# All first products of the 128 expert blocks ahead of all second products, and 384 gathered tokens in place of 320

## What is computed

```python
q = (xb @ w_query).reshape(PEER_BLOCK, PEER_HEADS, 2, PEER_HALF)
s = jnp.einsum('bhpd,phnd->bhpn', q, sub_keys)
...                                    # top 16 of 128 on each side, top 16 of their 256 sums
eid = e1 * PEER_NKEYS + e2             # 8 heads x 16 experts of 16384, per token
gate = jax.nn.softmax(best_s, axis=-1)
act = jax.nn.gelu(jnp.einsum('bd,bhkd->bhk', xb, expert_u[eid]), approximate=False)
return jnp.einsum('bhk,bhkd->bd', gate * act, expert_v[eid])
```

## Time and profile before

| | us |
|---|---|
| median of three runs | 3494.87 (3494.62 to 3495.22) |
| span of the profiled execution | 3500.7 |
| mixer and projections | 0 to 1197 |
| selection | 1197 to 1635 |
| gate matrices | 1635 to 1877 |
| first group and the others | 1877 to 3471 |
| final norm | 3471 to 3501 |

### The profile page before, as it was taken

One profiled execution on the slowest core, in us unless ns is written; L12 is line 12 of the kernel. 1 busy time (PEld: TensorE's weight loads), 2 busy tenths in 40 slices (PEclk: granted clock), 3 DMA queues, 4 the chain that ended last, 5 costly groups with the idle time before them and its releaser, 6 DMA issues.

```text
span 3500.7 us, 56614 instructions
## 1 busy us (share of the span) xinstructions
PE 3350.9 (96%) x21384; PEld 3291.5 (94%) x21384; DVE 2591.7 (74%) x4995; ACT 1018.7 (29%) x1349; POOL 977.2 (28%) x773
## 2 busy tenths in 40 slices
PE   6999999999998999998998899999999999999996
PEld 6999999899998999998997899999999999999996
DVE  5554444233343379999997899999999999999996
ACT  5742222321322232222543122222222222222222
POOL 0000000000000111111002555555555555555550
PEclk8999999999999999999999999999999999999998
DMA  2111011111322232334889999899998999999992
GB/s 105 40 45 36 29 36 64 68 48 42 141 85 73 89 107 102 106 112 136 266 266 307 333 337 328 318 327 326 338 329 317 327 327 340 328 321 321 329 326 104
DMA packets 304353, 698.46 MB, mean 200 GB/s; under 512 B 23873, under 2 KB 124225, under 8 KB 303201
## 3 DMA queue, kind: packets, MB, share of 16 engines
q0 software_dynamic: 98592, 362.97, 28.5%
q1 hardware_dynamic: 104112, 276.89, 23.3%
q10 hardware_dynamic: 101520, 56.89, 5.3%
...
## 4 chain that ended last, share of the span: by engine, by line
PE 77%; DVE 17%; DMA 2%; DVEq 2%; ACT 1%; issue 1%; ACTq 0%; SPq 0%; PEldq 0%
PE PS L1532 29%; PE PS L365 16%; PE PS L1515 14%; PE PS L1223 6%; PE PS L1253 5%; DVE HOTG L2052 3%; PE PS L1447 3%; PE PS L380 1%; DVE HOT L2048 1%; DVE HOT L2049 1%; DVE fold L1980 1%; DVE besti L1924 1%; DVE sc L1915 1%; DVE besti L1916 1%; DVEq L1978 1%
## 5 line engine op out<-in xcount | busy, mean ns | idle before, releaser
L1532 PE MATMUL PS<-AH,VH 128*128 128x368 f32 x2048 | 513.8, 332 | 20.4 <-DVE VL L2075 10.9
L1532 PE MATMUL PS<-AH,VL 128*128 128x368 f32 x2048 | 515.2, 332 | 0.0
L1532 PE MATMUL PS<-AL,VH 128*128 128x368 f32 x2048 | 509.7, 330 | 0.0
L746 POOL DMA_INDIRECT SLOT<-rows_u,EID x256 | 346.4, 1353 | 578.5 <-DVE XLF L2091 257.5
L746 POOL DMA_INDIRECT SLOT<-rows_v,EID x256 | 333.7, 1304 | 205.7 <-DVE SLOT L2082 167.5
L1532 PEld LDWEIGHTS PS<-AH,VH 128*128 128x128 f32 x2048 | 365.2, 189 | 22.7 <-DVE VL L2075 12.1
L1532 PEld LDWEIGHTS PS<-AL,VH 128*128 128x128 f32 x2048 | 366.2, 189 | 0.0
L1532 PEld LDWEIGHTS PS<-AH,VL 128*128 128x128 f32 x2048 | 365.8, 189 | 0.0
L2091 DVE SCALAR_TENSOR_TENSOR XLF<-SLOT,GA,XLF 128x1024 f32<-128x1024 f32 x256 | 328.0, 1281 | 0.5 <-DMA SLOT<-rows_v,EID 0.2
L1109 ACT ACTIVATE VH<-VRAW 128x512 fp32r<-128x512 f32 x256 | 157.8, 628 | 567.7 <-PE PS L1532 567.7
L2082 DVE SCALAR_TENSOR_TENSOR SLOT<-SLOT,XHF 128x1024 f32<-128x1024 f32 x256 | 312.6, 1221 | 3.3 <-DMA SLOT<-rows_u,EID 3.3
...
## 6 DMA issues: line engine op xcount, KB each, us to landing
RAW<-experts_u SPq DMA_DIRECT2D x128, 512.0 KB, 6.4
VRAW<-experts_v SPq DMA_DIRECT2D x256, 256.0 KB, 5.8
...
RAW<-weights SPq DMA_DIRECT2D x69, 512.0 KB, 3.6
...
```

Source lines behind the costliest of these rows:

```text
L746: pool.indirect_dma_start(out=SLOT[n % NSLOT][:, :], out_offset=None, in_=table, in_offset=bass.IndirectOffsetOnAxis(ap=ids, axis=0)).then ...
L1532: mm = pe.matmul(PS[:, 4 + 2 * (d % 2) + t, 0:CH], w[:, d % 2, c * P:c * P + P], x[:, c, t * CH:t * CH + CH], start=(c == 0 and n == 0), s ...
```

## The change

- The gathered tokens are now 384, three full tiles (NSP = 3); the half tile and all code for it go. The dense ones are 672, in halves of CH = 336. Selection still has nine tiles.
- All 128 u blocks come first: 75 in selection, 43 within the (now 84) steps of the gate stage (up to E1 = 118), 10 in a tail. All activations go to memory.
- Then come 128 units: 16 groups of GE = 8 blocks, with eight second products each. A unit accumulates eight blocks' products, 48 matmuls, before VectorE adds it to HID; three PSUM sets are in turn (SETS). The activations of a group are read back at its predecessor's start (load_raw), and the gates in four parts (load_gates), into buffers that alternate between AHR/ALR and the dense columns of XH/XL. One v block is now 1024 columns wide and takes RAW, WH and WL as a u block does.
- The low parts: GpSimd makes those of all u blocks and of the even units, VectorE those of the odd units.
- The rows are one sequence of 384 u rows and then 384 v rows (NROW). VectorE takes 24 of them in each of the last six tiles of selection (144), two in each gate step (168), 30 in the tail, 28 in each group but the last, and six in the last. SLOTs in turn: four up to the tail, six from there on. The weights are made for half the pairs at a time (GA_CUT).
- The sums of the gathered tokens are transposed in the last group, a tile at a time.
- The loops over groups are written out instead of being a loop in the program.

```diff
-GE = 4
+GE = 8
 NG = NKEYS // GE
-EARLY = 2
-LATE = GE - EARLY
-NE = NG * EARLY
-NSP = 2
-HALF = P // 2
-S0 = NSP * P
-T0 = S0 + HALF
+NSP = 3
+T0 = NSP * P
 ND = T - T0
...
-NSLOT = 5
-NTILE = NSP + 1 + -(-ND // P)
+NTILE = NSP + -(-ND // P)
 PRE = 2
-SEL_E = (4, 5, 5, 5, 5, 5, 5, 5, 5)
+SEL_E = (5, 5, 6, 10, 9, 10, 9, 10, 9)
...
+E1 = 118
...
+NROW = NSP * PAIRS
+TILE_ROWS = 24
+STEP_ROWS = 2
+TAIL_ROWS = (2, 4, 4, 8, 12)
+UNIT_ROWS = (4, 3, 4, 3, 4, 3, 4, 3)
...
+def slot_of(s):
+
+    if s < ROWS_E0:
+        return (L0, L1, QA, QB)[s % 4]
+    if s < ROWS_E1:
+        return (L0, L1, G0, N0)[s % 4]
+    if s < WIDE_FROM:
+        return (L0, L1, N0, N1)[s % 4]
+    return (L0, L1, N0, N1, N2, N3)[(s - WIDE_FROM) % 6]
...
+            def load_unit(n):
+
+                sp.wait_ge(e_lo, n - 1)
+                sp.dma_start(RAW[:, n % 2, :], u_blk[n] if n < NKEYS else v_blk[n - NKEYS]).then_inc(e_in[n % 2], 16)
...
+            for n in range(NKEYS):
+                load_unit(n + 2)
+                sp.wait_ge(e_gelu, n + 3)
+                sp.dma_start(act_dram[n], AS[:, n % 2, :]).then_inc(e_out[n % 2], 16)
+                if n == E1 - 1:
+                    for b in range(2):
+                        sp.wait_ge(w_out[b], 16 * ((NWB + 1 - b) // 2 + 1))
+                    sp.wait_ge(w_mm, NSTEP + 2)
+                    load_raw(0)
...
+            for n in range(NKEYS, UNITS):
+                g, d = divmod(n - NKEYS, KD)
+                if n + 2 < UNITS:
+                    load_unit(n + 2)
+                if g + 1 < NG:
+                    if d == 0:
+                        load_raw(g + 1)
+                    if d in (0, 1, 2, 3):
+                        load_gates(g + 1, d)
...
+            for s in range(NSTEP):
+                for m in range(E0 + 1, E1 + 1):
+                    if s == (e_end(m - 2) + 1 if m > E0 + 1 else 0):
+                        e_low(m)
+                gather_to(ROWS_E0 + STEP_ROWS * s + 4)
...
+            for n in range(NKEYS, UNITS):
+                if n + 1 < UNITS and n + 1 not in LOW_ON_DVE:
+                    e_low(n + 1)
+                gather_to(done + 6)
+                done += UNIT_ROWS[n % KD]
...
+            def v_unit(g, d):
+
+                n, slot = NKEYS + KD * g + d, d % 2
+                hi, lo, at_bank = a_hi(g), a_lo(g), 2 + 2 * SETS[d]
+                pe.wait_ge(e_lo, n + 1)
...
+                for c in range(GE):
+                    if d == 0 and c % 2 == 0:
+                        pe.wait_ge(a_low, GE // 2 * g + c // 2 + 1)
+                    for p, (w, x) in enumerate(((WH, hi), (WH, lo), (WL, hi))):
                         for t in range(2):
...
+            for n in range(NKEYS, UNITS):
+                g, d = divmod(n - NKEYS, KD)
+                last = g == NG - 1
+                if n + 1 in LOW_ON_DVE:
+                    v_low(n + 1)
+                if not last:
+                    if 1 <= d <= 4:
+                        a_gates(g + 1, d - 1)
+                    take(UNIT_ROWS[d])
+                    if d in (6, 7):
+                        for c in range(4 * (d - 6), 4 * (d - 6) + 4, 2):
+                            a_lows(g + 1, c)
...
+                dve.wait_ge(e_mm, n + 3)
+                part = halves(HID[:, d, T0:T])
+                dve.tensor_tensor(part, part, vset(d), ALU.add).then_inc(acc_done, 1)
```

762 lines of the change are left out of this document (299 added, 463 removed).

## The result

The changed kernel takes **3694.02 us** (median of 4 runs, 3686.71 to 3699.91) against 3495.05 us before (median of 4 beside it): a ratio of 1.0569, 95% interval 1.0554 to 1.0585. The forecast was 3402 us in a range of 3286 to 3490, so it missed in size and in sign. The profiled execution has a span of 3691.0 us. In the rows PE is TensorE, PEld its loading of weights, DVE VectorE, ACT ScalarE, POOL GpSimd; the clock is the one granted to TensorE, as a share of full speed.

What follows compares the result with a forecast made beforehand. TensorE was taken as the bound, with VectorE and DMA close behind. Selection's end 1815 + gates 466 + tail 88 + 15 groups x 62.9 + last group 60 + end 34 = 3407 us of span; forecast 3402, range 3286 to 3490.

Steps and rivals of the forecast that it cites:

- Narrower products: Dense products of 336 columns, not 368: 155.5 ns a matmul, not 168.4, relieving TensorE of 159 us.
- Selection: Stage from 1197 us on: TensorE sets it, VectorE hidden by 6 us a tile; 618 us, ending at 1815.
- Gate matrices: Stage of 84 steps and 43 u blocks: gathers' round trip decides, 5.55 us a step, 466 us.
- four resources: Gate stage: TensorE 413 us, VectorE 394, GpSimd 4.5 of 4.9 us a step, DMA 425 to 465 us.
- on average 1.2 us of a subtraction ahead of it on GpSimd: Gate stage: part of a gather's round trip, beside landing time, 0.6 us to see the slot free and 1.1 of use.
- Landing time: L, from a gather's issue to its landing: taken as 8.2 us, bounds 6.6 (no wait) and 10.
- The two conditions: Gate step takes (L + 2.9)/2 or 4.9 us if more; a pair of units in groups 14.9 or 6.9 + L.
- Rival C: Gathers' round trip in gate stage and odd units makes it slower: 3500 at L = 9.1, 3590 at 10; chance 0.16.
- Groups: Groups of eight second products: TensorE 59.7 us, VectorE 56.3, DMA 61 at 400 GB/s; 62.9 us each.
- rival B: Sustained memory rate only 357 GB/s: groups 68.3 us, gate stage 474, whole 3490 us; chance 0.10.
- The wait for the gates' reload: Once a group, VectorE's first gate product waits for 3.5 MB asked for late; 2 to 3 us left.
- Tail and last group: Ten u blocks after the gate stage, 88 us with 13 for TensorE's wait; last group without gathers, 60 us.

Runs made afterwards that it cites:

- x3: Changed kernel with GpSimd's subtraction covering 8 of the 1024 columns of its tile in every unit; 3596 us.
- x2: Changed kernel with the gate stage's 43 subtractions made by VectorE behind its step's rows, two steps later, instead of by GpSimd; 3570 us.
- x4: Changed kernel with GpSimd issuing each gate step's four gathers ahead of its subtraction; 3600 us.
- x13: Changed kernel with gate-stage and group subtractions on VectorE, gate products one unit later, rows spread more evenly over units, gate matrices stored as 16-bit floats; 3514 us.
- x12: x9 with each reload of gate matrices from the third group on bringing one block of the five or six; 3535 us.
- x14: x13 with the groups' v blocks asked for on ScalarE's DMA queue, one unit ahead, instead of on SyncE's; 3517 us.
- x9: Changed kernel with gate-stage and group subtractions on VectorE, and the groups' gate products and reloads one unit later; 3558 us.
- x7: Changed kernel with the groups' subtractions on VectorE and each gather of v rows bringing 2 KB a token instead of 4 KB; 3635 us.

## Why the prediction was wrong

- **Narrower products**: right. 153.8 ns a matmul for 155.5, so 179 us are off TensorE's products at full clock, for 159 forecast.
- **Selection** (forecast end 1815, measured 1872): the failed term is "24 gathered rows each at 1.14 us: 69 us", taken from rows that ran alone. Moving subtractions to GpSimd was counted as a relief of VectorE ("two weight subtractions (1.14 each) move to GpSimd"). Each cost it time instead: a tile took 85 us, of which x3 gives back 11. VectorE wasn't hidden by 6 us a tile, it set the pace (busy 409.5 of 425.6 us from 1446.4 to 1872). x3 shows it.
- **Gate matrices** (466, measured 596): VectorE's 4.69 us a step was exact, and so nearly was what four resources allow (x2: 476). The failed term is "on average 1.2 us of a subtraction ahead of it on GpSimd". The subtraction's length was in the sum and its wait for ScalarE was not: 207.4 us over 42 of them, up to 9.4 us each. I had asked who waits for the landing and not what the instruction ahead of the gathers waits for. x2 and x4 show it.
- **Landing time**: assumed 8.2, measured medians of 5.8 in the selection, 6.7 in the gate stage, 7.5 in the groups. The two conditions give 4.8 us a step ((L + 2.9)/2), under the floor of 4.9, and 14.4 us a pair (6.9 + L), under TensorE's 14.9: neither bound. Rival C got the sign and the place in the gate stage right, the gathers behind GpSimd's subtraction, but not the mechanism: the wait was for the start of that subtraction and not for a long landing.
- **Groups** (62.9, measured 67.6): two terms fell short. VectorE's "56.3 us" lacks four blockings of about 2.1 us: 64.6 busy. And DMA's 61 us stood on "the 400 GB/s that full slices reach": six good slices of 2.5 us. Such rates do last longer than a slice, but not for a group: 417 GB/s from 2851 to 2871 us, 394 from 3373 to 3423. The mean over long windows that rival B used was the better guide, 357 GB/s forecast, 365 to 370 measured at shares of 0.96 to 0.98. The wait for the gates' reload, put at 2 to 3 us a group, was right (30.7 us in twelve). Rival B's group (68.3) and gate stage (474, against 476 in x2 without the ring) were both close; I gave it 0.10. What it lacked to 3694 is the blocking and the ring. The Trainium skill's limit of about 358 GB/s for one core (DMA: Bandwidth & Descriptors, Specifications), which the prediction set beside that rival, is 2 to 3% below what these windows show.
- **Tail and last group**: 14 us each over the forecast. In the tail TensorE waited 18.7 us for low halves, where 13 were forecast for it, ScalarE once 16.3 us for a u block, and the granted clock was 0.90; in the last group it was 0.95. No run here takes these apart.

Where the gain went, then: 179 us less for TensorE's products at full clock; against them the blocking (x3: 72 us in the selection, 98 in all), the ring (x4: 84 us of the gate stage; x2: 123 with the blocking in it), and groups that carry 24.4 MB where the time of TensorE alone, 59.7 us, would hold 22 MB at 368 GB/s. With the ring gone, the gate products later and 16-bit gates it is still 0.7% behind the kernel before (x13).

**What stays open.** x12, x13 and x14 move 22.2 to 23.0 MB a group, which at 368 GB/s is 60 to 62.5 us, and VectorE has 60.7 us of work; yet the groups take 65 to 66 us, with DMA shares of 0.93 to 0.95 and 4.4 to 5.1 us a group in which VectorE waits, for v blocks in one, for rows in the other. Two resources at 0.93 each that wait for each other in turn would look so, but no run separates this from another cause. One that was left untested is VectorE's hold on GpSimd's gathers: in the changed kernel, from 2700 to 3500 us, those held for 1.9 us or more landed at a median of 10.7 us after their start, those of up to 1.2 us at 7.1. Nor does any tell whether memory or the 16 engines set the 365 to 370 GB/s, or whether they are a limit at all, with 394 over 50 us beside them. A packet of 4 KB takes 174 ns on average in x9's groups and 203 ns in x7's with its lighter traffic, so packets did not get longer with load; that speaks for the engines, but x7's packets are not the same ones.
